# Order of the dispatch tables, row transposes and shared product in a mixture-of-experts stage

## The reference, cut to what matters

```python
scores = jax.nn.sigmoid((t @ router_w).astype(jnp.float32))
_, idx = lax.top_k(scores + router_bias.astype(jnp.float32), TOP_K)      # TOP_K = 8 of N_EXPERTS = 64
sel = jnp.take_along_axis(scores, idx, axis=-1)
wts = sel / jnp.sum(sel, axis=-1, keepdims=True) * ROUTED_SCALE
gates = jnp.einsum('tk,tke->te', wts, jax.nn.one_hot(idx, N_EXPERTS, ...))
hid = jax.nn.silu(jnp.einsum('td,edf->tef', t, w_gate)) * jnp.einsum('td,edf->tef', t, w_up)
routed = jnp.einsum('tef,efd->td', hid * gates[..., None], w_down)
shared = (jax.nn.silu(t @ sh_gate) * (t @ sh_up)) @ sh_down
return (routed + shared).reshape(bsz, l, d)
```

## Time and profile before

| | us |
|---|---|
| Median of three runs | 1532.4 (1531.02 to 1533.92) |
| The profiled execution's own time | 1546.5 |
| Its span, first to last instruction | 1544.7 |
| The stage from the end of the last `shared_in` to the first `transpose_x` | 974.5 to 1011.2 |
| The blocks | 1011.2 to about 1460 |

### The profile page before, as it was taken

The page is one execution under the profiler, slowest core; times in us unless marked ns, Lnnn a source line. Parts: engine busy times, 40 slices in busy tenths (PEclk is TensorE's granted clock), DMA queues, the critical chain, the costliest instruction groups (busy, mean ns, idle before and its releaser), DMA issues. The chain is left out here.

```text
span 1544.7 us, 21871 instructions
## 1 busy us (share of the span) xinstructions
PE 1406.5 (91%) x8304; PEld 1049.5 (68%) x8304; DVE 699.3 (45%) x1267; ACT 415.9 (27%) x810; POOL 312.9 (20%) x450
## 2 busy tenths in 40 slices
PE   5999999999999999899798997899999999999664
PEld 1678776767898888455545546678888888888521
DVE  2657776402655664577565315442222222222255
ACT  2212021314645545333132012422222222222111
POOL 0200001002112210454353120021111111211172
PEclk9999799999999999999888898799999999999988
DMA  9645411129200000100111400189999999998695
GB/s 362 200 155 181 149 55 55 55 85 421 106 1 1 1 1 2 31 12 1 62 41 69 173 0 1 73 340 390 390 377 378 380 393 392 391 385 304 222 390 220
DMA packets 101058, 279.78 MB, mean 181 GB/s; under 512 B 22609, under 2 KB 39251, under 8 KB 99580
## 3 DMA queue, kind: packets, MB, share of 16 engines
q1 hardware_dynamic: 85148, 235.55, 41.6%
q0 software_dynamic: 15840, 43.28, 7.3%
HBM read 230.97 MB, written 64.52 MB: 191 GB/s over the span
## 5 line engine op out<-in xcount | busy, mean ns | idle before, releaser
L2672 PEld LDWEIGHTS PS<-arena 128*128 128x128 f32 x2240 | 258.0, 192 | 43.9 <-ACT arena L3160 27.2
L2672 PE MATMUL PS<-arena 128*128 128x128 f32 x2240 | 263.3, 276 | 4.9 <-DMA arena<-in_exp_w_down 3.5
L2976 DVE TENSOR_SCALAR arena<-PS,arena 128x1024 f32<-128x1024 f32 x70 | 89.9, 1284 | 141.5 <-PE PS L2680 141.5
L2680 PE MATMUL PS<-arena 128*128 128x512 f32 x280 | 137.8, 614 | 0.8 <-DVE arena L2969 0.8
L851 PE MATMUL PS<-arena 128*128 128x320 f32 x384 | 111.4, 445 | 1.5 <-DVE arena L1268 1.5
L856 PE MATMUL PS<-arena 128*128 128x320 f32 x384 | 107.3, 432 | 0.0
L3166 ACT ACTIVATE arena<-PS 128x128 f32<-128x128 f32 x70 | 19.4, 278 | 312.8 <-PE PS L2672 158.4
L2969 DVE TENSOR_TENSOR arena<-arena,PS 128x128 f32<-128x128 f32 x70 | 20.2, 288 | 183.0 <-ACT arena L3166 121.3
L851 PEld LDWEIGHTS PS<-arena 128*128 128x128 f32 x384 | 74.4, 196 | 33.1 <-issue 4.9
L856 PEld LDWEIGHTS PS<-arena 128*128 128x128 f32 x384 | 73.0, 190 | 30.4
L864 PE MATMUL PS<-arena 128*128 128x256 f32 (+1 forms) x400 | 89.7, 383 | 0.0
(11 more groups left out here) (467 smaller groups left out, 2184.6 us busy)
## 6 DMA issues: line engine op xcount, KB each, us to landing
arena<-in_exp_w_gate SPq DMA_DIRECT2D x70, 512.0 KB
arena<-in_exp_w_up SPq DMA_DIRECT2D x70, 512.0 KB
arena<-in_exp_w_down SPq DMA_DIRECT2D x70, 512.0 KB
y_rows<-arena SPq DMA_DIRECT2D x70, 512.0 KB
y_rows<-cst SPq DMA_DIRECT2D x1, 21504.0 KB, 58.4
arena<-in_w_in SPq DMA_DIRECT2D x16, 1024.0 KB, 6.2
arena<-in_w_mod SPq DMA_DIRECT2D x32, 512.0 KB, 3.6
arena<-in_w_mod SPq DMA_DIRECT2D x4, 2048.0 KB, 15.0
```

The source lines that it names most:

```text
L2672: mm = pe.matmul(PS[:, bank, 0:P], w[:, k, :], xT[j % 2][:, k, :], start=k == 0, stop=k == KT - 1)
L2680: mm = pe.matmul(PS[:, 4 + 2 * (j % 2) + half, :], hid[j % 2], ed[j][:, 512 * half:512 * half + 512], start=True, stop=True)
L2976: dve.tensor_scalar(yb[j].rearrange("p (h n) -> p h n", h=2), PS[:, 4 + 2 * (j % 2):6 + 2 * (j % 2), :], gate_col[j % 2], None, ALU.mult). ...
```

## The change

Instructions and operands stay the same in number and shape. What changes is their order on TensorE and ScalarE, and the banks of the shared second product. It is now written as `shared_down(n)` and goes to banks 0 to 3 in turn (`n % 4`), where the first products were. From n = 4 on, each waits for the copy of the one four before it (`s_acc >= n - 3`). The wait for all ten row copies is gone. ScalarE's copy is now `shared_out(n)`. VectorE's, GpSimd's and SyncE's lists are unchanged.

```diff
+                def shared_down(n):
+                    t, half = n // 2, n % 2
+                    if n == 0:
+                        pe.wait_ge(s_hid, 1)
+                    if n >= 4:
+                        pe.wait_ge(s_acc, n - 3)
+                    pe.matmul(PS[:, n % 4, :], shid[:, t * P:(t + 1) * P], ed[1][:, 512 * half:512 * half + 512],
+                              start=True, stop=True).then_inc(s_ps, 1)
...
                 shared_in(eu[1], 2, 1)
+                table(0)
                 row_transpose(4)
                 row_transpose(5)
-                table(0)
+                table(1)
+                shared_down(0)
+                shared_down(1)
                 row_transpose(6)
                 row_transpose(7)
-                table(1)
+                table(2)
+                shared_down(2)
+                shared_down(3)
                 row_transpose(8)
                 row_transpose(9)
-                table(2)
+                table(3)
                 pe.wait_ge(m_ecol, 1)
                 pe.matmul(PS[0:1, 7, 0:P], ecol, ident, start=True, stop=True).then_inc(m_erow, 1)
-                table(3)
+                shared_down(4)
+                shared_down(5)
                 table(4)
-
-                pe.wait_ge(b_cp, 2 * NT)
-                for n in range(2 * NT):
...
+                for n in range(6, 2 * NT):
+                    shared_down(n)
```

ScalarE:

```diff
                 for n in range(4):
                     row_copy(n)
+                token_block(0)
+                token_block(1)
                 act.wait_ge(s_gu, 2)
                 act.activation(sup..., PS[:, 2:4, 0:320], ACT.Copy).then_inc(s_up, 1)
-                for t in range(3):
-                    row_copy(4 + 2 * t)
-                    row_copy(5 + 2 * t)
-                    token_block(t)
+                row_copy(4)
+                row_copy(5)
+                token_block(2)
+                shared_out(0)
+                shared_out(1)
+                row_copy(6)
+                row_copy(7)
                 token_block(3)
+                shared_out(2)
+                shared_out(3)
+                row_copy(8)
+                row_copy(9)
                 token_block(4)
-                for n in range(2 * NT):
...
+                for n in range(4, 2 * NT):
+                    shared_out(n)
```

More of the change, by code:

```diff
@@ L3142, in _, with shared_out @@
                 act.activation(sact.rearrange("p (b n) -> p b n", b=2), PS[:, 0:2, 0:320], ACT.Silu).then_inc(s_act, 1)
+                def shared_out(n):
+                    t, half = n // 2, n % 2
+                    act.wait_ge(s_ps, n + 1)
+                    act.activation(acc[:, t, 512 * half:512 * half + 512], PS[:, n % 4, :], ACT.Copy).then_inc(s_acc, 1)
                 for n in range(4):
                     row_copy(n)
+                token_block(0)
+                token_block(1)
                 act.wait_ge(s_gu, 2)
                 act.activation(sup.rearrange("p (b n) -> p b n", b=2), PS[:, 2:4, 0:320], ACT.Copy).then_inc(s_up, 1)
-                for t in range(3):
-                    row_copy(4 + 2 * t)
-                    row_copy(5 + 2 * t)
-                    token_block(t)
+                row_copy(4)
[5 more added lines that the diff above has]
+                row_copy(7)
                 token_block(3)
+                shared_out(2)
+                shared_out(3)
+                row_copy(8)
+                row_copy(9)
                 token_block(4)
-                for n in range(2 * NT):
-                    t, half = n // 2, n % 2
-                    act.wait_ge(s_ps, n + 1)
-                    act.activation(acc[:, t, 512 * half:512 * half + 512], PS[:, 4 + half, :], ACT.Copy).then_inc(s_acc, 1)
+                for n in range(4, 2 * NT):
+                    shared_out(n)
                 def copy_xT(b, j):
```

## The result

The changed kernel takes 1523.32 us (median of 4 runs, 1523.14 to 1523.87) against 1531.99 us before: 8.7 us less, a ratio of 0.9939 with a 95% interval from 0.9923 to 0.9954 (7 to 12 us). Forecast were 1521.0 us, 11.4 us less. The profiled execution is one of the four runs, with 1523.87 us and a span of 1522.0 us.

What follows compares the result with a forecast made beforehand. TensorE was taken to wait on ScalarE's copies and mask scalings ahead of the tables, costing idle time and clock. Stage -14.9, gather +1.9 and clock +1.6 give -11.4 us, from 1532.4 to 1521.0 us; range 1516.5 to 1526.5.

Steps and rivals of the forecast that it cites:

- The waits: Stage ahead of the blocks: without waits and at full clock TensorE ends the tenth shared product 14.9 us earlier.
- The price of a table: Tables on TensorE: about 1.8 us each at full clock, against 3.63 to 3.72 us at half clock.
- What is late next: Gather of block 0: rows arrive 6.1 us behind the last table, costing 1.9 us; first transposes shift by -13.1 us.
- The clock behind the new pause: TensorE ahead of the first block: half clock for about 3.4 us, costing 1.6 us, between nothing and 5 us.
- The sum: Whole kernel: -14.9 for the stage, +1.9 for the gather, +1.6 for the clock, together -11.4 us.
- What cost nothing: Row and gate stores, weight loads of blocks 1 to 3 and new banks: 0 us; gate store with 0.5 us cover.
- A: Before the first block: gather hidden and clock stays up, -14.9 us or 1517.5 us; chance 0.16.
- B: Before the first block: gather lands at its latest and low clock lasts, -6.0 us or 1526.4 us; chance 0.14.
- E: Tables 0 to 2: another wait holds them and nothing changes, 1532.4 us; chance 0.03.
- C: Tables: clock stays low in them without any pause, leaving -3.7 us or 1528.7 us; chance 0.08.
- D: Blocks become bound by DMA, every `gate_up` 3.83 for 3.57 us, net +6.5 us or 1538.9 us; chance 0.03.

Runs made afterwards that it cites:

- tables_first_only: Kernel before with only tables 0 to 2 ahead of their row transposes and mask scalings moved accordingly, shared products whole behind the tables; ratio 0.9906 to the kernel before.
- before_filled: Kernel before with three extra matmuls of 128x512, results unread, ahead of each of tables 0, 1 and 2; ratio 0.9957 to the kernel before.
- after_filled: Changed kernel with three extra matmuls of 128x512, results unread, behind the last shared product; ratio 0.9896 to the kernel before, 1521.31 us.
- after: The changed kernel in its first timing and profile, against the kernel before; 1523.32 us, ratio 0.9939.
- after again: The changed kernel, unchanged, timed and profiled a second time; 1527.39 against 1536.78 us for the kernel before, ratio 0.9931.
- after_early: Changed kernel with only block 1's gate and up weights loaded early; ratio 0.9949 to the kernel before.
- six_behind: Changed kernel with shared products 4 and 5 also behind the last table, so six are there and not four; ratio 0.9925 to the kernel before.
- all_behind_gate: Changed kernel with all ten shared products behind the last table, tables 0 and 1 back to back, gates stored first; ratio 0.9933 to the kernel before.

## Why the prediction was right, and what it mis-sized

**The waits.** Right. The profile before put the pauses on L3138, and moving the mask scalings and tables took them away; tables_first_only shows that this is 14.3 of 15.3 us (1010.42 - 974.51 before, 990.48 - 969.87 after). The sum had 14.9.

**The price of a table.** Right: 1.77 us in the chain for 1.8. before_filled shows that the low clock hung on the pauses.

**What is late next.** Right: the gather, 6.03 us behind the table for 6.1, and the first transposes start 23.34 us behind the last first product. Before, it was 36.65 (1011.16 - 974.51), so the shift is -13.3 for -13.1. Neither end of the range was needed. The rule of the Trainium skill (DMA: Bandwidth & Descriptors, section "Anatomy of one DMA — SWDGE (gpsimd) path") would have it, as an estimate, at up to 7.6 us. The trace does not agree: in the changed kernel the last two packets over 2 KB of GpSimd's queue ahead of the landing fall between 992.5 and 992.6 us, and the rows are there at 993.07, so what follows the last of them was near 0.5 us, as the prediction chose.

**The clock behind the new pause.** Right in kind, mis-sized: the term of 1.6 us measured 2.6 (0.6 in the transposes, 1.96 in `gate_up`). The prediction let the low clock last 3.4 us, as from 978 to 982; it lasted from within 993 to 994 to within 1000 to 1001, about seven. All of that but 1.3 us was busy. after_filled gives 2.5 us by experiment, and the low clock stood behind this pause in all three profiles that have it unfilled (after, after again, after_early).

**The sum.** In the stage -15.3 + 2.0 + 2.6 = -10.7 us, against a forecast of -11.4. The timed -8.7 us, and -9.4 in the second series, have intervals that hold both. What is left between -10.7 and -8.7 cannot be assigned: in two profiles of the kernel before the last first product ended at 974.51 and at 965.61 us. That the stage came within 0.7 us of the forecast is in part luck, since two errors of the sum went opposite ways: the work and waits of TensorE gave 0.4 us more than was put down, and the clock took 1.0 us more.

**What cost nothing.** The row and gate stores: right here, but with the cover of 0.5 us named, which six_behind used up. The weights of block 1: right for the changed kernel (after_early). The reason given, that they keep their lead, was incomplete: after the change block 1's `gate_up` starts 14.0 us behind the tenth shared product, by the pause and the low clock, and before it started 9.5 us behind. In tables_first_only and all_behind_gate, where the first block follows as closely as before, 1.3 and 3.1 us of waiting for the weights came up. But before_filled waits 1.47 us with the same work behind the tenth product as the kernel before, which waits for nothing there in two profiles. So the weights land at different times behind the same issue: 11 to 13 us behind the tenth shared product in three kernels, within 10.2 us in six_behind and within 9.5 in before. Why stays open; no run changed the order of the loads alone.

**The rivals.** A and B did not come: the gather was in sight, and not at its latest. E did not come either: no other wait held the tables. C is refuted. D, blocks bound by DMA, did not come: from the third gate_up to the last `down` the blocks took 428 to 432 us in all kernels, whatever was gained ahead of them.

## What to carry to other kernels

When an engine's waits are removed from a chain of small steps, look for what had started early behind that chain, a gather or a weight load, and was hidden by its length; keep enough independent work behind the last step that starts it. Independent work is worth most where it covers the longest latency, not where it fills the first gaps: two products moved from ahead of the last table to behind it gave 3.3 us. And price a pause of TensorE by what follows it as well, since a pause of 2 to 3 us can be followed by half clock. Behind the one of 2.7 us ahead of the first block it was so each time, and cost 2.6 us. It is no rule: in the last blocks of the changed kernel's second profile TensorE waited 2.27 us for weights, the granted clock stayed at 1.00, and `gate_up` took 3.83 us.

## What the runs showed of the hardware that was not expected

Matmuls whose results nobody reads made the kernel faster: nine more before the tables 6 us in the timed runs (3.8 to 4.5 us up to the third gate_up), three in the pause before the first block 6 us (2.2 us). The same pauses of 0.73 and 1.29 us left `gate_up` at 3.81 us in five profiles and were followed by a granted clock of 0.50 in a sixth; what decides it is open. Weights of 1.5 MB, asked for together with 3 MB for two later blocks, landed up to 11.75 us after the issue of their last part, when their queue had moved twice their size.
